# A two-layer decoder step in split float32: who makes the first low parts, in what order the first product runs, and which banks the fourth takes

## What is computed

```
h = rmsnorm(x, g_mix[0])
a = h @ w_pw1 + b_pw1
u = a[..., :D_MODEL] * jax.nn.sigmoid(a[..., D_MODEL:])
ext = jnp.concatenate([hist.astype(u.dtype), u], axis=1)
v = depthwise convolution of ext over 31 tokens, + b_dw
```

## Time and profile before

| | |
|---|---|
| median of 3 runs | 1360.8 us (1360.73 to 1361.55) |
| the profiled execution | 1361.71 us |
| its span, first to last instruction | 1359.9 us |
| its mean granted TensorE clock | 0.996 |
| TensorE busy | 1335.1 us (98%), 11378 matmuls |
| VectorE busy | 813.0 us (60%) |
| ScalarE busy | 600.0 us (44%) |
| GpSimd busy | 721.4 us (53%) |

### The profile page before, as it was taken

The page is one execution under the profiler, slowest core; times in us unless marked ns, Lnnn a source line. Parts: engine busy times, 40 slices in busy tenths (PEclk is TensorE's granted clock), DMA queues, the critical chain, the costliest instruction groups (busy, mean ns, idle before and its releaser), DMA issues.

```text
span 1359.9 us, 26961 instructions
## 1 busy us (share of the span) xinstructions
PE 1335.1 (98%) x11378; PEld 1257.5 (92%) x11378; DVE 813.0 (60%) x1245; ACT 600.0 (44%) x1020; POOL 721.4 (53%) x504
## 2 busy tenths in 40 slices
PE   7999899999999999999999999999999999999998
PEld 7877499999999999999999977778999999999997
DVE  6688757554545453767666666665675454545534
ACT  5211456443434443444566644542464434343432
POOL 3322343587878785434232444420438888887831
PEclk9999999999999999999999999999999999999999
DMA  5654412233232323332111587760222222232222
GB/s 218 187 180 131 134 63 76 84 104 99 92 100 95 99 93 130 140 108 64 39 36 55 185 306 298 269 247 14 81 93 94 93 94 94 94 93 94 93 93 67
DMA packets 108360, 160.79 MB, mean 118 GB/s; under 512 B 7697, under 2 KB 93969, under 8 KB 102993
## 3 DMA queue, kind: packets, MB, share of 16 engines
q1 hardware_dynamic: 100688, 116.57, 26.7%
q0 software_dynamic: 7168, 41.95, 8.2%
q10 hardware_dynamic: 384, 0.55, 0.2%
HBM read 146.28 MB, written 4.03 MB: 111 GB/s over the span
## 4 chain that ended last, share of the span: by engine, by line
PE 94%; DVE 2%; DMA 1%; POOL 1%; ACT 1%; issue 0%; SPq 0%; DVEq 0%; POOLq 0%; ACTq 0%
PE ps L1734 33%; PE ps L1867 21%; PE ps L1855 19%; PE ps L1999 5%; PE ps L1772 2%; PE ps L2052 2%; PE ps L2096 2%; PE ps L1785 1%; PE ps L2171 1%; DMA kp<-cache_kpe,rows 1%; PE ps L2042 1%; PE ps L2087 0%; PE ps L2106 0%; POOL wl L596 0%; PE ps L2113 0%
## 5 line engine op out<-in xcount | busy, mean ns | idle before, releaser
L596 POOL TENSOR_TENSOR wl<-raw,wh 128x512 fp32r<-128x512 f32 (+2 forms) x249 | 430.9, 1733 | 419.4 <-ACT wh L727 419.2
L727 ACT ACTIVATE wh<-raw 128x512 fp32r<-128x512 f32 (+2 forms) x253 | 192.4, 762 | 358.1 <-PE ps L1734 167.3
L596 POOL TENSOR_TENSOR wl<-wuv,wh 128x512 fp32r<-128x512 f32 x104 | 134.3, 1303 | 48.5 <-ACT wh L727 48.5
L1867 PE MATMUL ps<-mh,wl 128*128 128x272 f32 x768 | 158.6, 288 | 0.0
L1867 PE MATMUL ps<-mh,wh 128*128 128x272 f32 x768 | 158.6, 288 | 0.0
L1867 PE MATMUL ps<-ml,wh 128*128 128x272 f32 x768 | 158.3, 288 | 0.0
L1734 PE MATMUL ps<-xh,wh 128*128 128x272 f32 x704 | 148.3, 292 | 10.0 <-DVE xl L1111 9.9
L1734 PE MATMUL ps<-xh,wl 128*128 128x272 f32 x704 | 145.4, 289 | 0.0
L1734 PE MATMUL ps<-xl,wh 128*128 128x272 f32 x704 | 145.1, 288 | 0.0
L1734 PEld LDWEIGHTS ps<-xh,wh 128*128 128x128 f32 x704 | 110.5, 189 | 14.9 <-POOL wl L596 9.8
L1867 PEld LDWEIGHTS ps<-ml,wh 128*128 128x128 f32 x768 | 120.3, 188 | 0.0
(11 more groups left out here) (317 smaller groups left out, 3006.0 us busy)
## 6 DMA issues: line engine op xcount, KB each, us to landing
raw<-w_up SPq DMA_DIRECT2D x32, 1024.0 KB, 5.4
raw<-w_down SPq DMA_DIRECT2D x32, 1024.0 KB, 5.1
raw<-w_pw SPq DMA_DIRECT2D x11, 1024.0 KB, 6.5
shifted<-ext SPq DMA_DIRECT2D x96, 66.5 KB, 2.1
raw<-w_o SPq DMA_DIRECT2D x4, 1024.0 KB, 5.2
raw<-w_dq SPq DMA_DIRECT2D x3, 1024.0 KB, 5.3
raw<-w_uq SPq DMA_DIRECT2D x4, 768.0 KB, 4.5
diag<-diags SPq DMA_DIRECT2D x6, 384.0 KB, 3.6
```

The source lines that it names most:

```text
L596: pf.tensor_tensor(weight(wl, u), weight_raw(u), f32(weight(wh, u)), ALU.subtract).then_inc(w_lo, 1)
L727: af.activation(weight(wh, u), weight_raw(u), ACT.Copy).then_inc(w_hi, 1)
L1867: m = tf.matmul(acc_of(u)[:, h, :], w[:, k, :], a[:, k0 + k, h * HALF:(h + 1) * HALF], start=(k0 == 0 and k == 0 and n == 0), stop=(k0 > 0 ...
```

## The change

VectorE makes the low parts of units 0, 1 and 2 (`first_low`): that of unit 0 ahead of all of x, that of unit 1 ahead of x's chunk 2, that of unit 2 ahead of the square of chunk 2. GpSimd starts with unit 3. ScalarE makes the high part of unit 2 after two squares in place of eight, and that of unit 3 ahead of the norm's root. TensorE's first product is a function of its own: in each chunk the two terms with `xh` come first, and only the third waits for `xl`. The norm's sums move from chunk 6 of product 1 to chunk 1 of product 2. Product 3 goes to banks 6 and 7, in which the sums were, and waits for the root in place of `gated(0)`.

```diff
@@ -401,7 +401,7 @@
         def bank_of(u):
-            return 4 if u == 2 else 2 * (units[u].out % 2)
+            return {2: 4, 3: 6}.get(u, 2 * (units[u].out % 2))
@@ -626,9 +626,7 @@
-            low(0)
-            pool.wait_ge(w_lo, 2)
-            low(2)
+            pool.wait_ge(w_lo, 3)
             low(3)
@@ -769,14 +767,14 @@
             for c in range(DC):
+                if c == 2:
+                    ahead(0)
                 square(x[:, c, :])
-            ahead(0)
+            ahead(1)
             root_of(D)
             act.wait_ge(s_con, 16)
             for c in range(DC):
-                if c == 0:
-                    ahead(1)
-                elif c < DC - 1:
+                if 0 < c < DC - 1:
                     squares_after(c - LATER)
                     ahead(2 * c)
                 gate_()
@@ -1145,12 +1143,21 @@
             dve.wait_ge(s_vec, 16)
+
+            def first_low(u):
+                if u > 0:
+                    dve.wait_ge(w_lo, u)
+                dve.wait_ge(w_hi, u + 1)
+                df.tensor_tensor(weight(wl, u), weight_raw(u), f32(weight(wh, u)), ALU.subtract).then_inc(w_lo, 1)
+
+            first_low(0)
             for c in range(DC):
+                if c == 2:
+                    first_low(1)
                 low(xl[:, c, :], x[:, c, :], xh[:, c, :], V("g_mix0", c))
-            dve.wait_ge(w_lo, 1)
-            dve.wait_ge(w_hi, 2)
-            df.tensor_tensor(weight(wl, 1), weight_raw(1), f32(weight(wh, 1)), ALU.subtract).then_inc(w_lo, 1)
             for c in range(DC):
+                if c == 2:
+                    first_low(2)
                 add_square(c == 0)
@@ -1709,7 +1716,9 @@
             def begin(u):
                 pe.wait_ge(w_lo, u + 1)
-                if units[u].out > 2:
+                if u == 3:
+                    pe.wait_ge(root, 1)
+                elif units[u].out > 2:
                     pe.wait_ge(freed, units[u].out - 1)
@@ -1803,10 +1812,22 @@
-            product(0, xh, xl, True)
-            product(1, xh, xl, norm_at=6)
+            def first_product(u, ah, al):
+                begin(u)
+                for k in range(DC):
+                    pe.wait_ge(hi, k + 1)
+                    for n, (w, a) in enumerate(((wh, ah), (wl, ah), (wh, al))):
+                        if n == 2:
+                            lo_()
+                        for h in range(2):
+                            m = tf.matmul(ps[:, bank_of(u) + h, 0:HALF], weight(w, u)[:, k, :], a[:, k, h * HALF:(h + 1) * HALF],
+                                          start=(k == 0 and n == 0), stop=(k == DC - 1 and n == 2))
+                m.then_inc(mm, 1)
+
+            first_product(0, xh, xl)
+            product(1, xh, xl)
             for c in range(1, DC):
-                product(2 * c, xh, xl, early_at=2 if c == EARLY + LATER else None)
+                product(2 * c, xh, xl, norm_at=1 if c == 1 else None, early_at=2 if c == EARLY + LATER else None)
                 product(2 * c + 1, xh, xl)
```

## The result

The changed kernel is **slower by 0.28%**: 1364.8 us against 1361.2, ratio 1.0028 (95% interval 1.0020 to 1.0036). I had forecast 1361.5, with 1359.5 to 1363.5 as the range. The sign of the step and the place were right, its size was not: 0.7 us forecast, 3.7 measured. The chance that I gave to slower by over 0.2% was 0.11. Run once more beside three of the experiments, the changed kernel gave 1.0024 (1.0013 to 1.0036).

A forecast was written before the change was run, and what follows sets the result against it. TensorE, with 94% of the chain, bounds the kernel. An early start is lost to later waits: +0.7 us at product 4, 0 after, put on the median of 1360.8 gives 1361.5 us; range 1359.5 to 1363.5.

The forecast's parts named there:

- Head start: Opening: VectorE makes unit 0's low part in 1.22 us instead of GpSimd's 2.35; TensorE starts at 8.15, 1.71 us earlier.
- my bracket: End of product 0: 15.72 if TensorE speeds up 3.3 us after its start, 16.4 if at 13.17 as before.
- Norm's sums: Sums in product 2: start at 23.09, 1.18 us later than before, after TensorE waits 0.65 for VectorE's squares.
- This term of the sum: Sigmoid's table load behind the first gate product: not counted; the sigmoid was put 0.76 us after that product's start.
- The collision: First sample taps meet GpSimd's low part of unit 4; second gate product at 36.40, TensorE waits 2.3 us, product 4 0.7 later.
- rival C: TensorE's clock falls in its wait ahead of product 4, making the kernel slower: 1364.3 or 1363.0 us; chance 0.14.
- the short form: Clock fall with a slow stretch as short as the opening's: 3.3 us, 1.5 lost, 1363.0 us.
- the long one: Clock fall like that at 165 to 175 us: 2.8 us lost, 1364.3 us.
- Behind product 4: Products 4 and 5 and taps go on as before; product 6's low part, 1.18 later, stays hidden by 1.7 us.
- rival B: First taps do not collide; product 4 gains 1.35, product 6 waits for its low part, 0.9 left: 1359.9 us; chance 0.22.

The follow-up runs named there:

- e10: Kernel before with the wait for the constants moved behind the high part of unit 3, so two waits precede the first sigmoid; ratio 1.0012.
- e2: Changed kernel with products 4 and 5 waiting only for the readers of the banks they write; ratio 1.0013, 1363.5 us.
- e5: e1 with VectorE making the second gate product ahead of the sample taps of chunk 0; ratio 0.9998 against the kernel before.
- e7: Changed kernel with 20 matmuls whose results are overwritten put ahead of product 4; ratio 1.0021 against the kernel before.
- e6: e5 with SP loading block 3 ahead of the first shift copies; ratio 0.9988 against the kernel before.
- e8: e1 with SP loading block 3 ahead of the first shift copies, sample taps still ahead of the second gate product; ratio 1.0009.
- e1: Changed kernel with ScalarE's wait for the constants moved ahead of the norm's root; ratio 1.0017 against the kernel before, 1363.9 us.
- e9: Changed kernel run again without an edit; ratio 1.0024, 1365.4 us against 1361.9 for the kernel before.
- e11: e7 with 26 filling matmuls in place of 20; ratio 1.0013 against the kernel before, 1363.5 us.
- e4: Kernel before with VectorE making the low parts of units 0 and 1 and the first product taking xh terms first; ratio 0.9989, 1360.3 us.

## Why the prediction was wrong, point by point

**Head start.** Forecast 8.15 for the first matmul, 8.57 in the profile; the weights' first half landed 0.45 later than in the profile before (ScalarE's first high part at 6.10, not 5.65), which is no part of the change: the eleven other profiles with VectorE first begin between 8.06 and 8.41, e10 (GpSimd first) at 10.25. Product 0 ended at 16.68, near the end of my bracket that I had given as the late one (16.4), since TensorE sped up near 13.1, about as before, and not 3.3 us behind its start. I took the other end as likeliest; in the profiles of e2, e5 and e7 product 0 ended at 15.84, 15.97 and 15.67, so both happen. The Trainium skill's rule on this ("TensorE: Matmul & The Clock Gate", Part 1: the number of slow matmuls varies between runs of one kernel) agrees with kernels whose first product is the same on TensorE: 12 slow matmuls in e7, 26 in e6. The two profiles of one and the same kernel, the changed one, do not differ in it (speed-up 4.6 and 4.7 us behind the first matmul).

**Norm's sums.** Forecast: late by 1.18, TensorE waiting 0.65. Measured: late by 2.03 (23.94), waiting 0.4. The chain was the one that I worked out (high part 16.94, low part 18.13, six squares in 4.53), only from a later start. e6 shows that the lateness costs no more than this wait.

This term of the sum was missing, not mis-sized: it stood at nothing without a reason, and measured 1.34 us at product 4. What it made of the wait, 3.2 us where I had 2.3, then brought the fall of the clock, 1.6 us more.

**The collision.** Right in place and kind: GpSimd ahead of the tap by 0.17 us (0.18 forecast), the next gate product 2.51 behind GpSimd's end (2.52 forecast). The Trainium skill's rule ("SBUF — State Buffer", Who interferes with whom: the instruction that comes first blocks the other for its whole length) and the trace agree: the tap takes 2.51 us here and ends 0.28 us behind GpSimd's instruction, where four taps without GpSimd took 1.42. e8 against e6 gives 2.9 us for it in time.

**The clock, rival C.** I gave 0.14 to a fall of the clock and said that it decides from a wait between 1.8 and 3.2 us; mine was 2.3. With the table load the wait became 3.2, and the clock fell: 1.6 us at products 4 and 5. Waits of 1.9 in e1 and e8 and of 1.96 in e5 left it at 1.00. So C came, by way of the term that I had missed; its price was nearer to the short form (1.5) than to the long one (2.8). But "it decides from a wait between 1.8 and 3.2" does not hold: in e9 and e11 the clock fell behind the wait of 1.8 us near 660. So the wait of 2.3 us that I forecast was no safe side either; no run has that wait.

**Behind product 4.** I wrote that product 6 would be ready 1.7 us before TensorE. In the changed kernel it was ready first, but by 0.9 us (57.6 against 58.5; block 3 took 8.5 us to land), and only because TensorE was late. But rival B's bound, the block 3 behind the shift copies, was real: as soon as the bank's wait goes (e5), 1.96 us of it reappear ahead of product 6.

**The numbers.** 0.7 forecast = 0.72 at product 4. Measured at product 4: 0.72 + 0.87 (late start of product 0 and slow matmuls) + 1.34 (table load) = 2.93, plus 1.6 (clock), less 0.8 given back: 3.7 in span. Without the table load and the clock 0.8 us of it would have been left, near my 0.7, but partly by luck: a late start of 0.87 against 0.8 given back.

**Not settled:** where most runs of e1 lost their clock, and how much of the median the clock's fall at products 4 and 5 is (the profiles say 1.6, the ratios of e9 and e11 1.5, with overlapping intervals). The spans of single profiles differ by 1 to 2 us for reasons outside the opening, so the times rest on the ratios and the places on the profiles.

## What to carry to other kernels

When an instruction is taken out from between two waits of ScalarE, look where the table load of the next function now stands: it may change sides with a wait at no change of any operation, and costs its 1.28 us where somebody waits. Keep exactly one wait ahead of a function's first use. Writing the late one of two waits first might serve as well; no run here tries it. And take a head start where it ends by itself (e4): moving the squares, the norm and the banks along with it made VectorE late for a bank that TensorE needed, and it took three more edits (e6) to come level with e4.

## What the runs showed of the hardware

- A TensorE wait of 3.2 us in dense work (3.5 from the last start to the next) was followed by some 3.4 us at half clock (0.57 granted over 4 us) soon after the matmuls had begun again, in both profiles of the changed kernel. Waits of 1.9 us at the same place (profiles of e1 and e8) and of 1.96 ahead of product 6 (e5) were not. A wait of 1.8 us near 660 us was not in the first profile of the changed kernel, and was in e9 and e11 (0.50 granted from 662 to 665 us in e9). Matmuls whose results are thrown away kept the clock up and delayed nothing that counted: product 4 stood 15.6 us behind the sums with and without them.
- TensorE's first speed-up came between 11.1 and 14.9 us into the span, not at a fixed distance from the first matmul: 4.6 us behind it in the changed kernel, 6.0 in e6, 2.9 in e7, 3.3 before.
- The same 1 MB block, with the same copies around it, landed 6.1 (e11) to 8.5 us (changed kernel) after its issue.
- An instruction with two waits ahead of it and a table load: the load ran behind the gate product's wait (30.60 us); with one wait it ran ahead of it (25.70 in e1).
